# A two-layer transformer kernel: position keys of latent attention made beside the dilated values, on token partitions, and transposed

## What is computed

```python
h = rms_norm(x, g_mix[l])
proj = h @ w_in[l]
c_q, c_kv, k_r, qkv_b, qkv_c, gate_logits = jnp.split(proj, IN_SPLITS, axis=-1)   # 256, 128, 32, 2304, ...
# mla_mixer
q = (rms_norm(c_q, g_q) @ w_uq).reshape(B, S, MLA_HEADS, MLA_NOPE_DIM + MLA_ROPE_DIM)
kv = (rms_norm(c_kv, g_kv) @ w_ukv).reshape(B, S, MLA_HEADS, MLA_NOPE_DIM + MLA_V_DIM)
k_rope = apply_rope(k_rope, cos, sin)          # one for all 8 heads, 32 numbers a token
s = (einsum(qn, k_nope) + einsum(qr, k_rope)) * scale
# dilated_mixer: q_b and k_b get apply_rope, values do not
```

## Time and profile before

| | us |
|---|---|
| median of 3 runs | 3371.29 (3369.94 to 3375.58) |
| profiled execution | 3367.59 |
| its span, first to last instruction | 3365.8 |
| TensorE busy | 3291.4 |
| VectorE busy | 1789.8 |
| ScalarE busy | 1316.7 |
| GpSimd busy | 600.9 |
| mean granted TensorE clock | 0.994 |

### The profile page before, as it was taken

One profiled execution on the slowest core, in us unless ns is written; L12 is line 12 of the kernel. 1 busy time (PEld: TensorE's weight loads), 2 busy tenths in 40 slices (PEclk: granted clock), 3 DMA queues, 4 the chain that ended last, 5 costly groups with the idle time before them and its releaser, 6 DMA issues.

```text
span 3365.8 us, 38576 instructions
## 1 busy us (share of the span) xinstructions
PE 3291.4 (98%) x15644; PEld 2730.1 (81%) x15644; DVE 1789.8 (53%) x2674; ACT 1316.7 (39%) x2018; POOL 600.9 (18%) x518
## 2 busy tenths in 40 slices
PE   8999999999999999999999999999999999999998
PEld 7788878888887887788888888888888888788887
DVE  6765574444437664755444455554444358854433
ACT  4643453332226533533223323333332238733321
POOL 1420131011003310220110022111111025531101
PEclk9999999999999999999999999999999999999999
DMA  4012223222221122222332322222223222223232
GB/s 137 32 67 79 88 82 117 94 100 97 97 94 57 58 70 79 104 82 94 100 100 97 101 79 85 85 88 82 94 93 103 94 75 89 90 68 106 94 100 82
DMA packets 85425, 296.92 MB, mean 88 GB/s; under 512 B 9472, under 2 KB 11776, under 8 KB 85248
## 3 DMA queue, kind: packets, MB, share of 16 engines
q1 hardware_dynamic: 85248, 294.47, 26.1%
HBM read 292.33 MB, written 2.10 MB: 87 GB/s over the span
## 4 chain that ended last, share of the span: by engine, by line
PE 84%; DVE 8%; ACT 4%; issue 2%; POOL 2%; DMA 0%; SPq 0%; POOLq 0%; DVEq 0%; ACTq 0%
PE bank L312 82%; PE bank L315 2%; DVE wl L554 2%; ACT wh L527 1%; POOL u_g L574 1%; DVE u_uc L550 1%; DVE small L1217 1%; POOL u_q L574 0%; DVE u_h L3092 0%; ACT c_k L527 0%; DVE m_ptl L554 0%; DVE m_qf L544 0%; ACT b_v L527 0%; POOL x L574 0%; ACT m_p L530 0%
## 5 line engine op out<-in xcount | busy, mean ns | idle before, releaser
L554 DVE TENSOR_TENSOR wl<-raw,wh 128x1024 fp32r<-128x1024 f32 (+1 forms) x532 | 686.3, 1293 | 871.8 <-ACT wh L527 868.7
L312 PE MATMUL bank<-zh,wh 128*128 128x512 f32 (+1 forms) x2668 | 1040.5, 390 | 15.0 <-ACT zh L527 7.2
L312 PE MATMUL bank<-zl,wh 128*128 128x512 f32 (+1 forms) x2668 | 1029.2, 386 | 5.6 <-DVE zl L557 5.5
L312 PE MATMUL bank<-zh,wl 128*128 128x512 f32 (+1 forms) x2668 | 1029.4, 386 | 3.4 <-DVE wl L554 3.4
L527 ACT ACTIVATE wh<-raw 128x1024 fp32r<-128x1024 f32 (+1 forms) x532 | 557.8, 1052 | 565.0 <-PE bank L312 505.9
L312 PEld LDWEIGHTS bank<-zh,wh 128*128 128x128 f32 x2668 | 505.2, 189 | 116.1 <-ACT zh L527 7.5
L312 PEld LDWEIGHTS bank<-zh,wl 128*128 128x128 f32 x2668 | 504.9, 189 | 108.8 <-DVE wl L554 7.3
L312 PEld LDWEIGHTS bank<-zl,wh 128*128 128x128 f32 x2668 | 505.1, 189 | 103.2 <-DVE zl L557 7.7
L312 PE MATMUL bank<-f_mh,wh 128*128 128x512 f32 (+1 forms) x748 | 284.7, 381 | 0.0
L312 PE MATMUL bank<-f_mh,wl 128*128 128x512 f32 (+1 forms) x748 | 282.8, 378 | 0.0
L312 PE MATMUL bank<-f_ml,wh 128*128 128x512 f32 (+1 forms) x748 | 281.7, 377 | 0.0
(11 more groups left out here) (340 smaller groups left out, 4485.0 us busy)
## 6 DMA issues: line engine op xcount, KB each, us to landing
raw<-in_wts SPq DMA_DIRECT2D x530, 512.0 KB, 3.3
c_nb<-in_c_bias SPq DMA_DIRECT2D x16, 384.0 KB, 3.1
x<-in_xT SPq DMA_DIRECT2D x8, 256.0 KB, 6.2
out<-x SPq DMA_DIRECT2D x16, 128.0 KB, 1.8
b_mask<-in_b_mask SPq DMA_DIRECT2D x2, 576.0 KB, 3.7
r_d<-in_decay SPq DMA_DIRECT2D x4, 256.0 KB, 2.7
raw<-in_wts SPq DMA_DIRECT2D x2, 256.0 KB, 3.2
m_t<-in_mla_tab SPq DMA_DIRECT2D x2, 256.0 KB, 5.0
```

The costliest lines, as they stand in the source:

```text
L312: return self.e.matmul(out, l, r, start=start, stop=stop, skip_group_check=inside)
L554: return self.e.tensor_tensor(out, src, b32(hi), ALU.subtract)
```

## The change

The order on TensorE becomes: low-rank tiles, dilated values, first dilated tiles, values of MLA. The fourth low-rank tile is gone. The 32 position columns of the keys ride as a fourth tile in the list of the dilated values, whose matmuls become 416 wide; so they come out with the tokens on the partitions. ScalarE copies them, scaled by the tokens' inverse root, to `m_kr` (four copies of 128x32), VectorE turns them there with four operations and repeats them four times (`vector_kr`), TensorE transposes four blocks of 128x128 into bank 4 (`turn`), and the high and low key rows are taken from that bank. GpSimd's product for the keys is gone. The tables for it are one load of 128x256 in place of two of 128x512.

Statistics, spread, squares and rows stand after steps 0, 2, 5 and 6 of the values. First keys, first queries and the transposes stand after steps 0, 1 and 3 of the first dilated tiles. The turns of the first two dilated tiles move from `mix` into MLA, to units 3 and 7. Banks are assigned anew. VectorE multiplies the latents by their rows before any turn.

```diff
-    a = [("a", l, j) for j in range(4)]
-    L.group(a, 8, L.z(*N), a_desc, range(4), [("ev",) + n for n in a])
-    b = [("b", l, 0, 0, w) for w in range(2)]
-    L.group(b, 8, L.z_whole(), b_desc, (4, 5), [("cp",) + n for n in b], {1: L.stat(N), 4: L.spread(N)})
+    a = [("a", l, j) for j in range(3)]
+    L.group(a, 8, L.z(*N), a_desc, range(3), [("ev",) + n for n in a])
...
+    tensor_bv(L, l, 0, {0: L.stat(N, 7), 2: L.spread(N), 5: squares, 6: rows})
...
-    tensor_bv(L, l, 0, {2: squares, 4: rows, 5: lambda: tensor_k(L, l, 0), 6: first_q})
+    def turn():
+
+        ps = L.claim(KR_BANK, "lo", "kr", l, 1)
+        L.wait_ge("ev", "kr", l)
+        for r in range(4):
+            t = L.tr(part(ps, r, 128), part(m.m_kr, 4 + r, 128))
+        t.then_inc(*L.tell("tp", "kr", l))
+
+    b = [("b", l, 0, 0, w) for w in range(2)]
+    L.group(b, 8, L.z_whole(), b_desc, (2, 7), [("cp",) + n for n in b], {0: lambda: tensor_k(L, l, 0), 1: first_q, 3: turn})
...
@@ scalar_bv
+        if p == 0:
+            L.cp(key_turn(m)[2][:, r, :], ps[:, 384:416], c).then_inc(*L.tell("cp", "krx", l, r))
@@ scalar_mix
-    for w in range(2):
-        scalar_b(L, ("b", l, 0, 0, w))
     L.ahead()
-    L.wait_ge("ev", "kr", l)
-    for i in range(2):
-        L.cp(m.m_k[i][0][64:128], m.m_qf[64:128]).then_inc(*L.tell("hi", "kr", l, i))
     L.wait_ge("ev", "nkv", l)
...
+    L.ahead()
+    scalar_bv(L, l, 0)
+    L.ahead()
     scalar_k_even(L, l, 0)
     scalar_k_odd(L, l, 0)
     scalar_q(L, l, 0)
-    scalar_bv(L, l, 0)
+    L.ahead()
+    L.wait_ge("tp", "kr", l)
+    for i in range(2):
+        L.cp(m.m_k[i][0][64:128], m.bank[KR_BANK][64:128]).then_inc(*L.tell("hi", "kr", l, i))
+    L.ahead()
+    for w in range(2):
+        scalar_b(L, ("b", l, 0, 0, w))
@@
+def vector_kr(L, l):
+
+    m = L.m
+    co, si, x, y = key_turn(m)
+    L.wait_ge("kct", "k", l)
+    L.wait_ge("cp", "krx", l, 3)
+    L.tt(y[:, :, 0:16], x[:, :, 16:32], si[:, :, 0:16], ALU.mult)
+    L.tt(y[:, :, 16:32], x[:, :, 0:16], si[:, :, 16:32], ALU.mult).then_inc(*L.tell("ev", "krs", l))
+    L.wait_ge("ev", "krs", l)
+    L.tt(x, x, co, ALU.mult).then_inc(*L.tell("ev", "krc", l))
+    L.wait_ge("ev", "krc", l)
+    four = [128, 4, 4, 32]
+    L.tt(m.m_kr[:, 512:1024].rearrange("p (r f d) -> p r f d", r=4, f=4), y.unsqueeze(2).to_broadcast(four),
+         x.unsqueeze(2).to_broadcast(four), ALU.add).then_inc(*L.tell("ev", "kr", l))
@@ vector_mix
-    vector_b_shift(L, ("b", l, 0, 0, 0))
     L.ahead()
     L.wait_ge("st", "q", l)
...
-    vector_b_add(L, ("b", l, 0, 0, 0))
-    vector_b_shift(L, ("b", l, 0, 0, 1))
-    for i in range(2):
-        L.wait_ge("hi", "kr", l, i)
-        L.lo(m.m_k[i][1][64:128], m.m_qf[64:128], m.m_k[i][0][64:128]).then_inc(*L.tell("lo", "kr", l, i))
-    vector_b_add(L, ("b", l, 0, 0, 1))
     L.wait_ge("st", "rkv", l)
-    L.tt(m.m_p[2], m.m_p[2], m.bank[5], ALU.mult).then_inc(*L.tell("ev", "nkv", l))
+    L.tt(m.m_p[2], m.m_p[2], m.bank[0], ALU.mult).then_inc(*L.tell("ev", "nkv", l))
...
+    L.ahead()
+    vector_kr(L, l)
+    vector_bv(L, l, 0)
+    L.ahead()
     vector_k_even(L, l, 0)
     vector_k_odd(L, l, 0)
     vector_q_turn(L, l, 0)
-    vector_bv(L, l, 0)
+    L.ahead()
+    L.wait_ge("hi", "kr", l, 1)
+    for i in range(2):
+        L.lo(m.m_k[i][1][64:128], m.bank[KR_BANK][64:128], m.m_k[i][0][64:128]).then_inc(*L.tell("lo", "kr", l, i))
@@ mla
+B_TURN = {3: (0, 0), 7: (0, 1), 11: (1, 0), 19: (1, 1), 27: (2, 0), 35: (2, 1)}
...
-        if i > 8 and i % 8 == 3:
-            vector_b_shift(L, ("b", l, 0) + MLA_FILL[i // 8 - 1])
-        if i > 8 and i % 8 == 4:
-            vector_b_add(L, ("b", l, 0) + MLA_FILL[i // 8 - 1])
+        if i in B_TURN:
+            vector_b_shift(L, ("b", l, 0) + B_TURN[i])
+        if i - 1 in B_TURN:
+            vector_b_add(L, ("b", l, 0) + B_TURN[i - 1])
```

More of the change, by code:

```diff
@@ L373, in steps, with turned @@
             yield
-    def turned(self, keys, nt, K, x, desc, banks, frees, extra={}):
+    def turned(self, keys, nt, K, x, desc, banks, frees, extra={}, width=None):
+        width = width or 128 * nt
         for k in range(K):
@@ L711, in a_desc @@
     _, l, j = n
-    cols = range(128 * j, 128 * j + 128) if j < 3 else list(range(384, 416)) * 4
-    return ("w_in", (l,), 128 * k, cols)
+    return ("w_in", (l,), 128 * k, range(128 * j, 128 * j + 128))
 def b_desc(n, k):
@@ L723, in desc @@
     def desc(j, k):
+        if j == 3:
+            return ("w_in", (l,), 128 * k, list(range(384, 416)) + [-1] * 96)
         o = B0 + 1536 + (4 * j + 2 * p) * 64
@@ L726, in bv_desc @@
     return desc
-BV_BANK = ((0, 1, 2, 3), (2, 1, 3, 0))
+BV_BANK = ((3, 4, 5, 6), (2, 1, 3, 0))
 def tensor_bv(L, l, p, extra={}):
     keys = [("bv", l, p, r) for r in range(4)]
-    L.turned(keys, 3, 8, L.z_tokens(), bv_desc(l, p), BV_BANK[p], [("lo",) + n for n in keys], extra)
+    L.turned(keys, 3 if p else 4, 8, L.z_tokens(), bv_desc(l, p), BV_BANK[p], [("lo",) + n for n in keys], extra,
+             384 if p else 416)
 def scalar_bv(L, l, p, rs=range(4)):
@@ L768, in b_bank @@
     _, l, p, g, w = n
-    return 4 + w if p == 0 and g == 0 else w if p else 0
+    return (2, 7)[w] if p == 0 and g == 0 else w if p else 0
 def vector_b_shift(L, n):
@@ L825, in rows @@
         L.wait_ge("pw", "q", l)
-        L.claim(5, "ev", "nkv", l)
-        L.rows(5, m.qcol[:, 4:8]).then_inc(*L.tell("st", "rkv", l))
-        L.claim(4, "ev", "nq", l, 1)
-        L.rows(4, m.qcol[:, 0:4]).then_inc(*L.tell("st", "rq", l))
+        L.claim(0, "ev", "nkv", l)
+        L.rows(0, m.qcol[:, 4:8]).then_inc(*L.tell("st", "rkv", l))
+        L.claim(1, "ev", "nq", l, 1)
+        L.rows(1, m.qcol[:, 0:4]).then_inc(*L.tell("st", "rq", l))
+    tensor_bv(L, l, 0, {0: L.stat(N, 7), 2: L.spread(N), 5: squares, 6: rows})
     def first_q():
@@ L846, in tensor_mix, with key_turn @@
         i.then_inc(*L.tell("mm", ("acc", "mv", l, t), *(L.spent(w) if t == 3 else [])))
+def key_turn(m):
+    return [part(m.m_kr, i, 128).rearrange("p (r d) -> p r d", r=4) for i in range(4)]
 def scalar_mix(L, l):
@@ L881, in vector_mix @@
     L.lead = 1
-    vector_stat(L, N)
+    L.wait_ge("st", "stat", *N)
+    L.ts(m.vtmp[:, 0:4], m.bank[7][:, 0:4], 1.0 / 1024, EPS, ALU.mult, ALU.add).then_inc(*L.tell("rv", *N))
     L.wait_ge("rr", *N)
-    for j in range(4):
+    for j in range(3):
         L.wait_ge("mm", "acc", "a", l, j)
-        L.tt(m.m_p[j] if j < 3 else m.m_qf, m.bank[j], m.rrow, ALU.mult).then_inc(*L.tell("ev", "a", l, j))
+        L.tt(m.m_p[j], m.bank[j], m.rrow, ALU.mult).then_inc(*L.tell("ev", "a", l, j))
     L.wait_ge("cp", "sqq", l, 1)
@@ L1031, in vector_q_turn @@
     L.wait_ge("rct", "t", l)
-    L.wait_ge(*(("pl", "ql", l, h - 1) if h else ("lo", "kr", l, 1)))
+    if h:
+        L.wait_ge("pl", "ql", l, h - 1)
     L.tt(m.m_qf, m.bank[q_bank(h)], m.m_t, ALU.mult).then_inc(*L.tell("ev", "q", l, h))
@@ L1247, in gpsimd_mla @@
             gpsimd_q(L, l, i // 4 + 1)
-        if i > 8 and i % 8 == 3:
-            gpsimd_b(L, ("b", l, 0) + MLA_FILL[i // 8 - 1])
+        if i in B_TURN:
+            gpsimd_b(L, ("b", l, 0) + B_TURN[i])
         if i >= 16 and i % 8 == 0:
@@ L3384, in constants @@
     one = np.ones((64, S), np.float32)
-    mla = np.stack([np.concatenate([one, cc, ss]) * np.float32(-MLA_SCALE), np.tile(cc, (4, 1)), np.tile(ss, (4, 1))])
+    mla = np.concatenate([one, cc, ss]) * np.float32(-MLA_SCALE)
+    key = np.concatenate([in_remainders(x).reshape(32, 4, 128).transpose(2, 1, 0).reshape(128, 128) for x in (cc, ss)], axis=1)
     c, s = rope_half(64, 10000.0)
```

51 lines of the change are left out of this document (19 added, 32 removed).

## The result

The changed kernel takes 3357.2 us (median of 4 runs, 3354.7 to 3359.5), the kernel before 3370.7 on the same chip (3369.9 to 3375.6): ratio 0.9954, 95% interval 0.9942 to 0.9966. That is 13.5 us less, 0.46%. The forecast was 3359.4 us, range 3352 to 3368, most likely faster by over 0.2%: it held.

A forecast was written before the change was run, and what follows sets the result against it. TensorE, busy 3291.4 of 3365.8 us, was taken as the bound. Matmuls -7.5, waits -6.0 and -3.0, new waits +1.4, turns in MLA +3.2 gave -11.9 us: 3359.4 us from a median of 3371.3, range 3352 to 3368.

The forecast's parts named there:

- Matmuls, -7.5: TensorE, both layers: fourth low-rank tile removed, values widened, four transposes added; net 3.73 us less per layer, 7.5 in two.
- Waits of layer 0, -6.0: Layer 0's stage before the first score matmul: 4.4 us idle, mainly awaiting the latent's low part, plus 1.6 slow clock, end.
- of layer 1, -3.0: Layer 1's stage before the first score matmul: 3.0 us idle ends, including late-split chunks of 1.10 and 1.17 us.
- The clock's price of 1.6 us: Layer 0, behind the 3.50 us wait: 15 matmuls take 4.4 us instead of 2.8 at the lower granted clock.
- New waits in the stage, +1.4: Per layer 0.7 us of new TensorE waits: 0.3 for the inverse root, 0.4 for the chunk wanted at 60.2.
- The walk: Step-by-step timing of layer 0's stage in the new order from 26.75 us, giving when each result is ready and needed.
- Turns in MLA, +3.2: Dilated turns moved to MLA units 3 and 7 cost 0.4 and 1.2 us, 1.6 per layer.
- (c): Rival: MLA's gaps swallow the turns and the stage's new waits do not come; -16.5 us, time 3354.8, chance 0.13.
- the 2 us allowance: Moved chunk boundaries shift chunk waits elsewhere, each 0.6 to 1.2 us, either sign; 2 us allowed each way.
- (b): Rival: chunks late in the values' steps, 1.1 us waits return, turns cost 1.6 each; -4.3 us, 3367.0, chance 0.26.
- (d): Rival: VectorE bounds MLA's first units, turns cost 4.8 us each, slower from 3.8; +4.1 us, 3375.4, chance 0.11.
- (a): The whole kernel as forecast, -8 to -16 us; chance 0.50.

## Why the prediction was right, point by point

**Matmuls, -7.5.** Held. 24 matmuls given back cost 5.4 us (layer 1), the wider values cost what the interpolated 0.000415 us per column says, and the next matmul starts 0.35 us after the four transposes, at 57.97, its successor 0.32 behind it instead of 0.23: 0.44 us in all, as taken.

**Waits of layer 0, -6.0, of layer 1, -3.0.** Held in kind, and for the reason given: moving the two turns alone gives 4.7 and 3.2 us. The clock's price of 1.6 us was somewhat high for the stage: with TensorE busy over the wait, the stretch behind it lost 1.1 (and there stood idle for 0.2 us at 73.58, which slower matmuls had filled). The sizes were short. With the 3.73 us of matmuls and the new 0.60 taken out, 9.74 - 3.73 + 0.60 = 6.6 us came back in layer 0 and 7.10 - 3.73 + 0.60 = 4.0 in layer 1, 1.6 more than forecast. Part of it is that the first step after a wait is longer (behind the wait of 1.43 us the starts lie at 123.35 and 123.70, 0.35 us apart instead of 0.23); the rest isn't accounted for.

**New waits in the stage, +1.4.** Measured 0.60 in each layer, so +1.2, but all of it at the inverse root (forecast 0.3), and none for the chunk at 60.2 (forecast 0.4). GpSimd took 2.55 us for the root instead of the 2.03 of the earlier trace rows. The walk's other instants, less the 0.42 us by which the first matmul came later, were: values step 0 ends at 28.95 (forecast 29.0), the root is ready at 46.4 (45.8), the low part at 49.6 (48.7), VectorE's key operations at 55.1 (54.2), the transposes start at 57.2 (56.4), unit 0 at 65.9 (65.5). The low part and the rotated keys had more slack than their errors. The small copies were the bound least known, 0.1 to 0.6 us; the row shows 0.34 for one, and the next copy starts 0.17 us after it, near the 0.25 taken.

**Turns in MLA, +3.2.** The size was near (+2.1) by luck, for the mechanism was another. With the chunks' old boundaries the turns cost between nothing (113.53 against 113.65) and 0.3 us (113.80 against 113.48) per layer: the gaps hold them, as rival (c) had it. What lengthened MLA is that the chunks' boundaries fall on other units; whether they would do so without the moved turns beside them is open. The prediction saw that the boundaries move, and gave the move 2 us of either sign without saying where. The place where it expected to see the turns, the wait for the queries' turn after unit 7 (1.25 us at 107.46), shrank to 0.39 in the changed kernel, and another grew to 1.43. The rule of the Trainium skill, "SBUF — State Buffer", section "Who interferes with whom", would have made the four turns cost 7.0 us; its kind is seen (the division at 1.22 us instead of 0.69), its price is not: the four turns cost at most some tenths of a us where the boundaries stayed.

**Elsewhere.** The chunk wait at 855.81, +1.2, is the 2 us allowance at work, and the shifted chunks show that it is that. The first matmul at +0.42 is no effect of the change that could be told: it starts at 7.24 and 7.73 us in the two executions of before, at 7.66 and 7.99 in those of the changed kernel.

**The rivals.** (b) fell: no chunk is late in the values' steps. (d) fell: nothing near 3.8 us per turn. (c) was right on the turns and wrong on the walk, which kept its 0.6 us, so the sum stayed at (a): -11.9 forecast, -12.9 in the spans, -13.5 in the medians. The sum is nearer than its terms: the waits gave 1.6 us more than forecast, the turns' term and the new waits cost 1.3 us less, and stretches to which it gave nothing cost 1.8 (0.42 + 1.15 + 0.24).

## What to carry to other kernels

Price TensorE's work by the spacing of starts, and a wait by what stands ahead of its releaser on that engine; then take the work out of the stage, for putting it last there only passes the wait on to whoever needs what was behind it (11 us here). Where weights come in chunks, another order of the tiles or another length of their lists moves every later boundary: compare the list of waits of a stage that the edit doesn't touch before blaming the edit. And where several waits of 1 to 3 us stand in a row, removing one is worth its idle time, but what the clock gives back (1.1 us here) is lost among the falls that differ from one execution to the next. Before reading a stretch of one profile to tenths of a microsecond, look at a second execution of the same kernel.

## What the runs showed of the hardware

**The clock falls behind some waits and not behind others, and not always behind the same.** Windows of the same stretch, right behind the wait for b_v, in two executions of the changed kernel; first the one above (wait 1.57 us):

```profile
184.30:190.80 6.50, 6.50 (x26) 5.07 (x24) 2.49 (x6) 1.55 (x4) 0.91 (x1) 0.74 0.23 81
```

and the second (wait 1.48 us):

```profile
184.30:190.80 6.50, 5.49 (x28) 4.17 (x27) 2.63 (x7) 1.90 (x4) 0.90 (x1) 1.00 0.24 81
...
1077.00:1080.00 3.00, 3.00 (x9) 2.35 (x8) 2.12 (x6) 1.24 (x4) 2.83 (x3) 0.50 0.02 5
```

In the first the clock is at its lower level, 1.2 GHz, for about half of the stretch, yet only 2 of 28 matmuls are lost, since the second execution stands idle for 1.01 us at 188.63 that the slower matmuls of the first fill. A clock of 0.50 puts starts of 128x512 matmuls 0.42 to 0.43 us apart (80.79 to 81.21 above, 0.42) instead of 0.2266. The second execution has no fall near 184 and 1136 us, where the first has them, and falls at 456.5, 1077.0, 2708 and 2759.4, where the first has none. So a few us of a run, and the difference between two profiles of one kernel, are a matter of where the falls come; what decides that stays open.

**The first matmuls of a run stand as far apart as at the lower clock, for a time that differs.** Up to 13.4 us in the first execution of before and 11.2 us in the second, 13.8 and 11.6 us in those of the changed kernel, 128x512 matmuls start 0.43 us apart, and 0.23 from there on; the window's clock says 1.00 on both sides. No wait shows between them. From the first matmul to the values' steps it takes 37.19 and 35.98 us in before, 19.47 and 18.41 in the changed kernel. The stage lengths of layer 0 in the experiments are read with this in mind.

**GpSimd's small operation took longer behind a longer idle time.** The same operation on 128x8 numbers took 2.03 us after 1.30 us idle (before, both layers), 2.14 after 4.6 and 5.7 us (two turns moved), and 2.55 after 9.7 to 14.8 us (the changed kernel, the squares sooner, the wide values, the latents first). Two things speak against a plain rule: 1.64 us after 12.5 us idle, in layer 1 of the kernel with the chunks shifted, and the same operation on 128x4 numbers, 1.86 to 1.92 us after 30 to 138 us idle. So the 0.5 us by which the prediction missed the root came with GpSimd's other work no longer standing ahead of it; why is open.
